# The first weight-block sum of an FFN Strassen pair, taken from VectorE and made by an adding DMA of GpSimd

## The chip, the core and the metric

The kernel runs on one core of a Trainium2 chip, in one launch. The metric is the device time in microseconds; the time before is the median of three runs.

## What is computed

One layer of a diffusion backbone over 512 latent tokens of width 2048 (float32): adaLN-modulated RMSNorm, an input projection into an S5 branch and a Hyena branch, their merge and the output projection, then the SwiGLU FFN, and a last RMSNorm. The change is in the FFN:

```python
def swiglu(h, w_in, w_out):
    a, b = jnp.split(h @ w_in, 2, axis=-1)
    return (jax.nn.silu(a) * b) @ w_out
...
        x = x + gate_mix[:, None] * mixer_output(u_x, y_x, hy_x, gates_x, lp)
        x = x + gate_ffn[:, None] * swiglu(modulate(x, norm_ffn[l], shift_ffn, scale_ffn),
                                           w_ffn_in[l], w_ffn_out[l])
```

## The kernel before

The work is written engine by engine, one function each for SP, GpSimd (POOL), ScalarE, VectorE and TensorE, with semaphores between them; the order on an engine is the order of its code. Every weight stands twice in a matmul: as a high half, rounded to fp32r by ScalarE, and as a low half, the difference, made by VectorE.

The first product of the FFN has 44 tiles of 128 columns for the gate (a) and as many for the up side (b). Tiles 0 to 2 are done plainly, the other 41 (`N_PAIR`) as **pairs**: gate and up tile of one number, cut with the 2048 rows of the contraction in halves, are a 2 x 2 grid of weight blocks of 128 x 1024 elements (512 KB), multiplied with a 2 x 2 grid of activation blocks by Strassen's scheme in Winograd's form, with seven block products in place of eight. A pair p so needs seven weight operands. Blocks 0, 1, 2 and 3 are loaded, and four sums are made of them:

- sum one, block 4 = block 3 + block 2 (L2097)
- sum two, block 3 = block 0 - block 3, in place (L2101)
- sum three, block 5 = block 4 - block 0 (L2104)
- sum four, block 6 = block 1 - block 5 (L2109)

`PRODUCTS = (0, 4, 5, 1, 3, 6, 2)` gives the block of each of the products 0 to 6. The seven operands of a pair lie in a ring of twelve buffers `wx`; `x_free(p, j)` is the count of finished products (`w_used`) from which the buffer of block j of pair p is free.

Who does what, while TensorE runs product i of pair p (o = 7p + i):

- **TensorE**, `pair_product` (L2839 to L2854): eight tiles of the contraction, for each a matmul of 512 columns with the high half (L2851) and one of 256 with the low half (L2853). It waits for the low half (`w_lo`) and, where a PSUM bank is used again, for ScalarE's copy of it.
- **ScalarE** makes the high half three products ahead (`operand_hi`, L1264), copies the banks of products 0, 1, 2 and 4 to SBUF (`chain_copy`, L1276), the last half bank of a pair (`up_half_copy`, L1281), and the SiLU (`pair_silu`, L1287).
- **VectorE** makes the low half two products ahead (`operand_lo`, L2115), and after it, at products 1 to 4, the four sums for pair p + 1 (`weight_sum`). In pair 0 the sums for pair 1 are at products 2, 3, 4 and 5. It also adds the banks up (L2122 to L2138), makes the low halves of the activation block sums `T` at the start (L2085), and at product 5 of pairs 0 to 31 does one row of the adaLN matrix (`ada_row`, L1651), which has nothing to do with the pairs.
- **SP** loads the blocks 3, 0, 2, 1 of a pair in this order (`pair_weights`, L596), each when its buffer is free and the sums of the pair before that read its own block of this number are done (`x_sum`). In the steady state these are the ends of products 2, 3, 5 and 6 of the pair two before.
- **POOL** multiplies SiLU and up side of a finished pair (`pair_product`, L812), stores the product to HBM (`store_act`, L806) and loads a row for `ada_row` when VectorE has done one (`ada_in`, L668), one after the other for each tile g.

In what follows T0 is the time at which product 0 of a pair starts.

Of the kernel before, what the change touches and what calls it, by code (L numbers as in the profile page):

```python
# [64 lines left out]
N_PLAIN = 3  # L65
N_PAIR = TILES - N_PLAIN
# [15 lines left out]
A_TILE = (0, 1, 3, 2)  # L82
# [16 lines left out]
MUL, ADD, SUB = ALU.mult, ALU.add, ALU.subtract  # L99
# [26 lines left out]
def block_kernel(nc, vecs_d, w_ac_d, w_ar_d, w_in_d, w_glu_d, w_hy_d, w_out_d, w_fi_d, w_fo_d, x_d, ctx_d,  # L126
# [5 lines left out]
    def at(name, off_kb, shape, dt=F32):  # L132
        return nc.alloc_sbuf_tensor_at(name, shape, dt, offset=base + int(off_kb * kb))
# [128 lines left out]
    wx = [at(f"wx{j}", o, [P, HU]) for j, o in enumerate(x_at)]  # L262
# [29 lines left out]
    def sem(name):  # L292
        return nc.alloc_semaphore(name)
# [1 line left out]
    s_vec, s_par, s_filt, s_dec, s_f3w, s_ctx = (sem(n) for n in  # L295
        ("vec_loaded", "s5a_loaded", "filter_loaded", "decay_loaded", "f3w_loaded", "ctx_loaded"))
    s_id, s_row = sem("ident_loaded"), sem("square_rows_ready")
    s_x, s_tabf = [sem(f"x_or_block_weight_loaded{g}") for g in range(4)], [sem(f"tabf_loaded{c}") for c in range(2)]
    s_pos = sem("postab_loaded")
    am_in = [sem(f"ada_mix_loaded{j}") for j in range(3)]  # L300
    am_used, am_row, am_cmb, ada1_used = (sem(n) for n in
# [3 lines left out]
    w_ld = [sem(f"hw_loaded{s}") for s in range(4)]  # L305
    w_hi, w_lo, w_used = sem("hw_hi_ready"), sem("hw_lo_ready"), sem("hw_used")
# [33 lines left out]
        "tf_loaded_or_xacc_moved", "tg_loaded_or_act_or_xacc_loaded"))  # L340
    tb_hi, tb_lo = sem("table_hi_ready"), sem("table_lo_ready")
    ut_ps, ut_h, ut_l = sem("uT_psum"), sem("uT_hi_ready"), sem("uT_lo_ready")
    pq_ps, pq_ev, k_in = sem("spec_psum"), sem("spec_free"), [sem(f"kf_in{j}") for j in range(2)]
    yv, yh, yl = sem("Y_ready"), sem("Y_hi_ready"), sem("Y_lo_ready")
    cv_ps, cv_out, od_cp, oh, ol = (sem(n) for n in ("conv_psum", "conv_gated", "odd_copied", "hyo_hi_ready", "hyo_lo_ready"))

# [6 lines left out]
    wz_free, x_sum = sem("pair_out_ready"), sem("h_or_weight_sum_ready")  # L353
# [23 lines left out]
    def ffn_slice(n):  # L377

        return w_fi_d[n - N_HU]

    def slot(n):

        return n % 3 if n < N_HU else (3, 1, 2, 0)[(n - N_HU) % 4]

    def x_buffer(p, j):

        return (7 * p + RING[j]) % 12

    def x_free(p, j):

        b = 7 * p + RING[j]
        if b < 12:
            return {1: N_HU + 9, 5: N_HU + 9, 6: N_HU + 10}.get(b, N_W if b > 6 else 0)
        return N_W + 7 * ((b - 12) // 7) + PRODUCTS.index(RING.index((b - 12) % 7)) + 1
# [63 lines left out]
    for c, x, i in D_FILL:  # L458
        n, blocked = DOWN.index((c, x, i)), CHUNKS[c][2]
        if not blocked or PRODUCTS[i] < 4:  # L460
            j = PRODUCTS[i] if blocked else n % 4
# [26 lines left out]
    w_loads = [sum(slot(i) == j for i in range(N_W)) for j in range(4)]  # L488

    with nc.Block() as block:  # L490
        @block.sync
        def _(sp):
# [64 lines left out]
            n = H_MRG + 2 * N_FILL  # L557
# [7 lines left out]
            def ffn_weights(n):  # L565

                if n == N_HU:
                    sp.wait_ge(m_sum, KT)
                else:
                    sp.wait_ge(w_used, n - 3)  # L570
                sp.dma_start(hw_raw[slot(n)][:, :], ffn_slice(n)).then_inc(w_ld[slot(n)], 16)

            def down_weights(n):

                c, x, i = DOWN[n]
                j, count, last = d_load[n]
                sp.wait_ge(w_used, d_free(n))
                landed = s_x[j] if CHUNKS[c][2] else w_ld[j]
                if last is None and not CHUNKS[c][2]:
                    sp.wait_ge(x_sum, 4 * N_PAIR + 4)  # L580
                if last is not None and CHUNKS[c][2]:
                    sp.wait_ge(x_sum, d_sums(*DOWN[last][:2]) + (2, 4, 1, 1)[j])
                if last is not None and not CHUNKS[c][2]:
                    sp.wait_ge(w_hi, N_D + last + 1)
                row = D_ROWS.index((c, x, (0, 1, 3, 2)[j] if CHUNKS[c][2] else i))
                sp.dma_start(dw[d_buffer(n)][:, 0:d_width(n)], w_fo_d[row][:, 0:d_width(n)]).then_inc(landed, 16)

            def pair_weights(p, j):

                if x_free(p, j):  # L590
                    sp.wait_ge(w_used, x_free(p, j))
                if p:
                    sp.wait_ge(x_sum, 4 * p + (2, 4, 1, 1)[j])
                else:
                    sp.wait_ge(w_hi, (N_W, N_W - 2, N_W - 1, N_W - 3)[j])
                sp.dma_start(wx[x_buffer(p, j)][:, :], w_fi_d[4 * (N_PLAIN + p) + A_TILE[j]]).then_inc(w_ld[j], 16)  # L596
# [5 lines left out]
                    ffn_weights(N_HU)  # L602
            for n in range(N_HU + 1, N_W):
                ffn_weights(n)
            for p in range(N_PAIR):
                for j in ((3, 0, 2, 1) if p else (3, 1, 2, 0)):
                    pair_weights(p, j)
            for c, (k0, nk, blocked) in enumerate(CHUNKS):
                for x in range(KT // 2 if blocked else KT):
                    for i in ([PRODUCTS.index(j) for j in (3, 0, 2, 1)] if blocked else [i for cc, xx, i in DOWN if (cc, xx) == (c, x)]):  # L610
                        down_weights(DOWN.index((c, x, i)))
# [8 lines left out]
        def _(pool):  # L620
# [4 lines left out]
            for st in range(8):  # L625
                cs, f, half = 1 - st // 4, st // 2 % 2, st % 2
# [181 lines left out]
            def pair_product(p):  # L808
# [2 lines left out]
                pool.wait_ge(wz_free, 2 * p + 2)  # L811
                pool.tensor_tensor(f_s[:, :], f_s[:, :], u_sum[:, :], MUL).then_inc(ft_rd, 1)  # L812

            def load_act(c, part):

                k0, nk = CHUNKS[c][0:2]
                a, b = 4 * part, min(4 * part + 4, nk)
                pool.dma_start(a_raw[:, a:b, :], act_d[:, k0 + a:k0 + b, :]).then_inc(act_in[part], 16)
# [12 lines left out]
            for g in range(TILES - 1):  # L831
                if g == TILES - 2:
                    stored(7)
                    pool.wait_ge(w_used, N_D - 6)
                    load_act(0, 0)
                if g >= N_PLAIN:
                    pair_product(g - N_PLAIN)
                store_act(g)
                if 2 <= g < 32:
                    ada_in(N_WIDE + g)  # L840
# [566 lines left out]
        def _(dve):  # L1407
# [127 lines left out]
            a, b, c, e, r = (rt6[:, j, :] for j in range(5))  # L1535
# [344 lines left out]
            for q in range(4):  # L1880
                n = H_MRG + 3 * q
# [50 lines left out]
            n, row = H_MRG + 2 * N_FILL, N_GATE  # L1932
# [59 lines left out]
            for m in range(KT):  # L1992
                n = H_OUT + 2 * m
# [93 lines left out]
            def operand(p, j):  # L2087

                return wx[x_buffer(p, j)][:, :]

            def weight_sum(p, e):

                if e == 0:
                    dve.wait_ge(w_ld[2], 16 * (w_loads[2] + p + 1))
                    dve.wait_ge(w_ld[3], 16 * (w_loads[3] + p + 1))
                    dve.wait_ge(w_used, x_free(p, 4))
                    tt(operand(p, 4), operand(p, 3), operand(p, 2), ADD).then_inc(x_sum, 1)  # L2097
                if e == 1:
                    dve.wait_ge(w_ld[0], 16 * (w_loads[0] + p + 1))
                    dve.wait_ge(x_sum, 4 * p + 5)  # L2100
                    tt(operand(p, 3), operand(p, 0), operand(p, 3), SUB).then_inc(x_sum, 1)  # L2101
                if e == 2:
                    dve.wait_ge(w_used, x_free(p, 5))
                    tt(operand(p, 5), operand(p, 4), operand(p, 0), SUB).then_inc(x_sum, 1)  # L2104
                if e == 3:
                    dve.wait_ge(w_ld[1], 16 * (w_loads[1] + p + 1))
                    dve.wait_ge(w_used, x_free(p, 6))
                    dve.wait_ge(x_sum, 4 * p + 7)
                    tt(operand(p, 6), operand(p, 1), operand(p, 5), SUB).then_inc(x_sum, 1)  # L2109
# [151 lines left out]
            for o in range(7 * N_PAIR):  # L2261
                p, i = o // 7, o % 7
                if o in (1, 3):
                    h_sums_lo((3, 1)[o // 2])
                if o + 2 < 7 * N_PAIR:
                    if p + 1 < N_PAIR and i == 5 and p == 0:
                        weight_sum(1, 3)
                    operand_lo(o + 2)
                else:
                    down_lo(o + 2 - 7 * N_PAIR)  # L2270
                e = i - 1 if p else i - 2
                if p + 1 < N_PAIR and 0 <= e < 4 and not (p == 0 and e == 3):
                    weight_sum(p + 1, e)
                if i == 0 and p == 33:
                    dve.wait_ge(ada1_used, 8 * KT)
                if p and i == 0:
                    up_folds(p - 1)
                if i == 4:
                    gate_sum(p, 0)
                if i == 5:  # L2280
                    if p < 32:
                        ada_row(N_WIDE + p)
                    if p == N_PAIR - 1:
                        for k in range(4):
                            act_lo(0, k)
                    up_sum(p)
                if i == 6:
                    gate_sum(p, 1)
                    gate_fold(p)
                if o == 1:  # L2290
                    ffn_product(2)
# [4 lines left out]
            for n, (c, x, i) in enumerate(DOWN):  # L2296
# [24 lines left out]
                if c < N_XC:  # L2321
                    e = n - D_FIRST[c] - 11
# [777 lines left out]
```

## Time and profile before

| what | us |
|---|---|
| median of 3 runs (lowest, highest) | 2776.66 (2776.16, 2777.51) |
| time of the profiled execution | 2776.75 |
| its span | 2774.9 |
| TensorE busy (share) | 2730.1 (98%) |
| VectorE busy | 2169.9 (78%) |
| ScalarE busy | 1141.0 (41%) |
| GpSimd busy | 371.1 (13%) |

The span runs from the first to the last instruction, the time is that of the whole execution. A busy share says how long an engine worked, not whether anything waited for it. That is in the waits, in the idle times before groups of instructions, and in the timelines of the engines side by side. HBM reads are 428 MB, writes 44 MB, 170 GB/s over the span.

### The profile page before, as it was taken

How to read it: one execution, taken by the hardware profiler on the slowest of the kernel's cores; microseconds unless marked ns; L12 is line 12 of the kernel's file. 1: busy time of each engine (PE TensorE's matmuls, PEld its weight loads, DVE VectorE, ACT ScalarE, POOL GpSimd, SP SyncE). 2: the span in 40 equal slices, each digit the busy share in tenths (PEclk: the TensorE clock that was granted, in tenths of full speed). 3: DMA queues.
4: the chain of work that ended last, by engine and by line, in shares of the span. 5: the costliest groups of instructions: out<-in, count | busy, mean ns of one | idle time of the engine just before them, and what ended most of it. 6: DMA issues, size and time to landing. Idle time of an engine off the chain costs nothing.

```text
span 2774.9 us, 39621 instructions
## 1 busy us (share of the span) xinstructions
PE 2730.1 (98%) x15602; PEld 2313.4 (83%) x15602; DVE 2169.9 (78%) x2986; ACT 1141.0 (41%) x1701; POOL 371.1 (13%) x544
## 2 busy tenths in 40 slices
PE   7999999999999999999999999999999999999998
PEld 2688888888888888788788888888888888998997
DVE  6555676887885685666789999999999887776877
ACT  4332333223443532222245555555555554453542
POOL 0001331001333100001100111111111111000001
PEclk9999999999999999999999999999999999999999
DMA  9736985346775645767644444444444336434432
GB/s 403 323 95 150 190 191 143 115 129 192 225 226 180 240 135 181 232 223 264 218 159 141 153 147 154 144 155 145 152 141 129 123 115 212 143 92 151 137 103 96
DMA packets 144540, 475.27 MB, mean 171 GB/s; under 512 B 24993, under 2 KB 29489, under 8 KB 140130
## 3 DMA queue, kind: packets, MB, share of 16 engines
q1 hardware_dynamic: 85570, 300.90, 33.7%
q0 software_dynamic: 49760, 157.67, 18.2%
q10 hardware_dynamic: 9024, 14.16, 1.4%
q8 instruction: 124, 2.03, 0.3%
q14 instruction: 62, 0.51, 0.1%
HBM read 428.14 MB, written 44.44 MB: 170 GB/s over the span
## 4 chain that ended last, share of the span: by engine, by line
PE 88%; DMA 5%; DVE 3%; ACT 2%; issue 1%; POOL 1%; SPq 0%; ACTq 0%; POOLq 0%; DVEq 0%
PE ps L2851 19%; PE ps L2555 11%; PE ps L2557 11%; PE ps L2556 11%; PE ps L2853 10%; PE ps L2902 3%; PE ps L2901 3%; PE ps L2900 3%; PE ps L2879 2%; PE ps L2880 2%; PE ps L2881 2%; PE ps L2572 2%; PE ps L2532 1%; DMA hw_raw<-in_w_in 1%; DMA hw_raw<-in_w_glu 1%; PE ps L2599 1%
## 5 line engine op out<-in xcount | busy, mean ns | idle before, releaser
L1416 DVE TENSOR_TENSOR hw_lo<-hw_raw,hw_hi 128x1024 fp32r<-128x1024 f32 x220 | 269.1, 1224 | 320.2 <-ACT hw_hi L870 319.0
L870 ACT ACTIVATE hw_hi<-hw_raw 128x1024 fp32r<-128x1024 f32 x220 | 232.5, 1058 | 683.2 <-DMA hw_raw<-in_w_in 463.3
L2851 PE MATMUL ps<-t_hi_lo,wx_hi 128*128 128x512 f32 x1312 | 412.0, 395 | 0.0
L2115 DVE TENSOR_TENSOR wx_lo<-wx,wx_hi 128x1024 fp32r<-128x1024 f32 x287 | 351.4, 1224 | 41.7 <-ACT wx_hi L1264 37.2
L2555 PE MATMUL ps<-h_hi,hw_hi 128*128 128x512 f32 x896 | 354.0, 395 | 0.7 <-DVE st_a L1680 0.5
L2557 PE MATMUL ps<-h_hi,hw_lo 128*128 128x512 f32 x896 | 349.4, 390 | 0.0
L2556 PE MATMUL ps<-h_lo,hw_hi 128*128 128x512 f32 x896 | 348.8, 389 | 0.0
L1264 ACT ACTIVATE wx_hi<-wx 128x1024 fp32r<-128x1024 f32 x287 | 302.1, 1053 | 105.3 <-PE ps L2853 98.2
L2851 PE MATMUL ps<-h_hi_lo,wx_hi 128*128 128x512 f32 x984 | 309.0, 395 | 0.0
L2853 PEld LDWEIGHTS ps<-t_hi_lo,wx_lo 128*128 128x128 f32 x1312 | 246.5, 188 | 58.3
L2853 PE MATMUL ps<-t_hi_lo,wx_lo 128*128 128x256 f32 x1312 | 257.7, 278 | 0.0
L2853 PEld LDWEIGHTS ps<-h_hi_lo,wx_lo 128*128 128x128 f32 x984 | 184.8, 188 | 43.7
L1313 ACT ACTIVATE dw_hi<-dw 128x768 fp32r<-128x768 f32 (+1 forms) x192 | 144.4, 753 | 157.8 <-PE ps L2881 126.8
L2851 PEld LDWEIGHTS ps<-t_hi_lo,wx_hi 128*128 128x128 f32 x1312 | 199.7, 189 | 0.0
L2169 DVE TENSOR_TENSOR dw_lo<-dw,dw_hi 128x768 fp32r<-128x768 f32 (+1 forms) x192 | 162.0, 845 | 48.0 <-ACT dw_hi L1313 47.2
L2555 PEld LDWEIGHTS ps<-h_hi,hw_hi 128*128 128x128 f32 x896 | 168.2, 188 | 37.3 <-issue 2.8
L2557 PEld LDWEIGHTS ps<-h_hi,hw_lo 128*128 128x128 f32 x896 | 168.2, 188 | 35.7
L2556 PEld LDWEIGHTS ps<-h_lo,hw_hi 128*128 128x128 f32 x896 | 168.4, 188 | 33.7
L2853 PE MATMUL ps<-h_hi_lo,wx_lo 128*128 128x256 f32 x984 | 193.3, 278 | 0.0
L2901 PE MATMUL ps<-blk_lo_hi,dw_hi 128*128 128x256 f32 x672 | 190.2, 283 | 0.0
L2902 PE MATMUL ps<-blk_lo_hi,dw_lo 128*128 128x256 f32 x672 | 190.2, 283 | 0.0
L2900 PE MATMUL ps<-blk_lo_hi,dw_hi 128*128 128x256 f32 x672 | 190.2, 283 | 0.0
(430 smaller groups left out, 5688.9 us busy)
## 6 DMA issues: line engine op xcount, KB each, us to landing
wx<-in_w_fi SPq DMA_DIRECT2D x164, 512.0 KB, 3.6
hw_raw<-in_w_in SPq DMA_DIRECT2D x128, 512.0 KB, 4.8
ada1m<-in_w_ar POOLq DMA_DIRECT2D x96, 512.0 KB, 4.7
ada_mix<-in_w_ac SPq DMA_DIRECT2D x16, 2048.0 KB, 13.0
dw<-in_w_fo SPq DMA_DIRECT2D x80, 384.0 KB, 3.1
ada1g<-in_w_ar POOLq DMA_DIRECT2D x32, 512.0 KB, 5.5
hw_raw<-in_w_glu SPq DMA_DIRECT2D x32, 512.0 KB, 4.5
hw_raw<-in_w_out SPq DMA_DIRECT2D x32, 512.0 KB, 4.5
```

What stands on the lines that cost most here:

```text
L870: act.activation(hw_hi[slot(n)][:, :], hw_raw[slot(n)][:, :], ACT.Copy).then_inc(w_hi, 1)
L1264: act.activation(wx_hi[o % 4][:, :], wx[x_buffer(p, j)][:, :], ACT.Copy).then_inc(w_hi, 1)
L1416: tt(hw_lo[s][:, :], hw_raw[s][:, :], hw_hi[s][:, :].bitcast(F32), SUB).then_inc(w_lo, 1)
L2115: tt(wx_lo[b][:, :], wx[b][:, :], wx_hi[o % 4][:, :].bitcast(F32), SUB).then_inc(w_lo, 1)
L2555: mm(out, wh(k), xh[:, k0 + k, :], start=first and k == 0, stop=False)
L2556: mm(out, wh(k), xl[:, k0 + k, :], start=False, stop=False)
L2557: ins = mm(out, wl(k), xh[:, k0 + k, :], start=False, stop=last and k == nk - 1)
L2851: mm(out[:, :], wh[:, P * k:P * k + P], both[:, :, k, :], start=opens and k == 0, stop=False, skip_group_check=True)
L2853: ins = mm(out[:, 0:CW], wl[:, P * k:P * k + P], xh[:, k, :], start=False, stop=k == ST - 1, skip_group_check=True)
L2900: mm(out, wh[:, w], b_hi[j][:, k, :], start=opens and k == 0, stop=False, skip_group_check=True)
L2901: mm(out, wh[:, w], b_lo[j][:, k, :], start=False, stop=False, skip_group_check=True)
L2902: ins = mm(out, wl[:, w], b_hi[j][:, k, :], start=False, stop=k == K_S - 1, skip_group_check=True)
```

## The change

Sum one of the pairs 1 to 40 leaves VectorE. SP loads block 2 a second time, into the buffer of block 4 (`first_addend`), behind the four blocks of the pair. POOL, when that has landed, issues a DMA of block 3 from HBM that adds to the same buffer (`second_addend`), ahead of the pair product and the store in its order. VectorE, where sum one stood, waits for that DMA and counts `x_sum` up itself. Blocks 2 and 3 are still loaded as before. Sums two to four of pairs 2 to 40 stand one product later, as they already did for pair 1. Two semaphores that were done with are used again.

```diff
+            def first_addend(p):
+
+                sp.wait_ge(w_used, x_free(p, 4))
+                sp.dma_start(wx[x_buffer(p, 4)][:, :], w_fi_d[4 * (N_PLAIN + p) + A_TILE[2]]).then_inc(s_tabf[0], 16)
+
             for p in range(N_PAIR):
                 for j in ((3, 0, 2, 1) if p else (3, 1, 2, 0)):
                     pair_weights(p, j)
+                if p:
+                    first_addend(p)
...
+            def second_addend(p):
+
+                pool.wait_ge(s_tabf[0], 16 + 16 * p)
+                pool.dma_start(wx[x_buffer(p, 4)][:, :], w_fi_d[4 * (N_PLAIN + p) + A_TILE[3]], accum_op=ADD).then_inc(k_in[1], 16)
+
...
+                if N_PLAIN - 1 <= g and g - N_PLAIN + 2 < N_PAIR:
+                    second_addend(g - N_PLAIN + 2)
                 if g >= N_PLAIN:
                     pair_product(g - N_PLAIN)
                 store_act(g)
...
             def weight_sum(p, e):
 
-                if e == 0:
+                if e == 0 and p:
+                    dve.wait_ge(w_ld[3], 16 * (w_loads[3] + p + 1))
+                    dve.wait_ge(k_in[1], 128 + 16 * p)
+                    dve.sem_inc(x_sum, 1)
+                if e == 0 and p == 0:
...
-                e = i - 1 if p else i - 2
+                e = i - 2
```

VectorE in pair 1, from the low half of product 3 on, before (`wx_lo` rows are low halves, `wx` rows are sums for pair 2, buffer numbers behind the names):

```order
L2115 TENSOR_TENSOR wx_lo_264<-wx_252,wx_hi_269 128x1024 [waits hw_hi_ready]
L2097 TENSOR_TENSOR wx_246<-wx_248,wx_249 128x1024 [waits hw_used,hw_loaded3,hw_loaded2]
L2115 TENSOR_TENSOR wx_lo_265<-wx_253,wx_hi_270 128x1024 [waits hw_hi_ready]
L2101 TENSOR_TENSOR wx_248<-wx_245,wx_248 128x1024 [waits h_or_weight_sum_ready,hw_loaded0]
L2115 TENSOR_TENSOR wx_lo_256<-wx_244,wx_hi_267 128x1024 [waits hw_hi_ready]
L2104 TENSOR_TENSOR wx_250<-wx_246,wx_245 128x1024 [waits hw_used]
L2115 TENSOR_TENSOR wx_lo_266<-wx_254,wx_hi_268 128x1024 [waits hw_hi_ready]
L2109 TENSOR_TENSOR wx_251<-wx_247,wx_250 128x1024 [waits h_or_weight_sum_ready,hw_used,hw_loaded1]
```

The same place in the changed kernel, where L2133 is the low half, L2119, L2122 and L2127 are sums two to four:

```order
L2133 TENSOR_TENSOR wx_lo_264<-wx_252,wx_hi_269 128x1024 [waits hw_hi_ready]
L2133 TENSOR_TENSOR wx_lo_265<-wx_253,wx_hi_270 128x1024 [waits hw_hi_ready]
L2133 TENSOR_TENSOR wx_lo_256<-wx_244,wx_hi_267 128x1024 [waits hw_loaded3,kf_in1_or_sum_added,hw_hi_ready]
L2119 TENSOR_TENSOR wx_248<-wx_245,wx_248 128x1024 [waits h_or_weight_sum_ready,hw_loaded0]
L2133 TENSOR_TENSOR wx_lo_266<-wx_254,wx_hi_268 128x1024 [waits hw_hi_ready]
L2122 TENSOR_TENSOR wx_250<-wx_246,wx_245 128x1024 [waits hw_used]
L2140 TENSOR_TENSOR gate_sums<-gate_sums,ps 128x512 [waits hw_used,ffn_a_copied_or_silu]
L2133 TENSOR_TENSOR wx_lo_257<-wx_245,wx_hi_269 128x1024 [waits hw_hi_ready,dve_chain]
L2127 TENSOR_TENSOR wx_251<-wx_247,wx_250 128x1024 [waits h_or_weight_sum_ready,hw_used,hw_loaded1]
```

The wait for the adding DMA (`kf_in1_or_sum_added`) now stands ahead of the low half of product 5, and each of the three sums behind one more low half.

POOL in the changed kernel, in three tiles of the steady state (L824 is the adding DMA, L819 the pair product, L813 the store, L675 the row load):

```order
L824 DMA wx_248<-in_w_fi 128x1024
L819 TENSOR_TENSOR ffn_silu<-ffn_silu,ct_201 128x512
L813 DMA act<-ffn_silu 128x512
L675 DMA ada1m_190<-in_w_ar 128x1024
L824 DMA wx_243<-in_w_fi 128x1024
L819 TENSOR_TENSOR ffn_silu<-ffn_silu,ct_201 128x512
L813 DMA act<-ffn_silu 128x512
L675 DMA ada1m_189<-in_w_ar 128x1024
```

Before, the rows were the same without L824: the adding DMA stands between the row load and the pair product.

## Rows read from the trace of the kernel before

**Rows 1.** Windows: us; busy (instructions) per engine; clock; DMA share; GB/s

```profile
core 0: us, PE busy (x) PEld busy (x) DVE busy (x) ACT busy (x) POOL busy (x), PEclk, DMA share, GB/s
1500.00:2298.00 798.00, 798.00 (x4584) 696.21 (x4583) 747.03 (x764) 418.71 (x540) 114.27 (x113) 1.00 0.44 144
```

**Rows 2.** Page, costliest groups: xcount | busy us, mean ns | idle before

```profile
L2851 PE MATMUL ps<-t_hi_lo,wx_hi 128*128 128x512 f32 x1312 | 412.0, 395 | 0.0
...
L2853 PE MATMUL ps<-t_hi_lo,wx_lo 128*128 128x256 f32 x1312 | 257.7, 278 | 0.0
```

**Rows 3.** Timeline of ScalarE in pair 21: start us, us, instruction [idle before <-releaser]

```profile
1908.29 0.38 ACT L1281 ACTIVATE up_half<-ps 128x256 f32<-128x256 f32 x1 [1.73 <-PE ps L2853]
...
1911.08 0.60 ACT L1276 ACTIVATE gate_sums<-ps 128x512 f32<-128x512 f32 x1 [0.94 <-PE ps L2853]
1911.57 1.05 ACT L1264 ACTIVATE wx_hi<-wx 128x1024 fp32r<-128x1024 f32 x1
1913.86 0.60 ACT L1276 ACTIVATE ct<-ps 128x512 f32<-128x512 f32 x1 [1.24 <-PE ps L2853]
...
1916.65 0.60 ACT L1276 ACTIVATE gate_sums<-ps 128x512 f32<-128x512 f32 x1 [1.24 <-PE ps L2853]
...
1922.22 0.60 ACT L1276 ACTIVATE ct<-ps 128x512 f32<-128x512 f32 x1 [1.73 <-PE ps L2853]
...
1927.80 0.38 ACT L1281 ACTIVATE up_half<-ps 128x256 f32<-128x256 f32 x1 [1.73 <-PE ps L2853]
```

**Rows 4.** Timeline of VectorE in pair 21

```profile
1909.65 1.23 DVE L2115 TENSOR_TENSOR wx_lo<-wx,wx_hi 128x1024 fp32r<-128x1024 f32 x1 [0.40 <-ACT wx_hi L1264]
1910.80 2.31 DVE L2097 TENSOR_TENSOR wx<-wx,wx 128x1024 f32<-128x1024 f32 x1
1913.04 1.21 DVE L2115 TENSOR_TENSOR wx_lo<-wx,wx_hi 128x1024 fp32r<-128x1024 f32 x1
1914.17 1.21 DVE L2101 TENSOR_TENSOR wx<-wx,wx 128x1024 f32<-128x1024 f32 x1
...
1922.36 1.28 DVE L1651 CUSTOM_DVE_ANT_0 ada1m<-ada1m,silu_row_m,mod_x 128x1024 f32<-128x1024 f32 x1
1923.57 0.08 DVE L1651 DVE_READ_ACCUMULATOR2_ANT mod_x<- 128x1 f32 x1
1923.57 0.69 DVE L2131 TENSOR_TENSOR ct<-ct,ct 128x512 f32<-128x512 f32 x1
1924.29 1.22 DVE L2115 TENSOR_TENSOR wx_lo<-wx,wx_hi 128x1024 fp32r<-128x1024 f32 x1
...
1925.43 0.68 DVE L2122 TENSOR_TENSOR gate_sums<-gate_sums,ps 128x512 f32<-128x512 f32 x1
1926.14 0.69 DVE L2126 TENSOR_TENSOR gate_sums<-gate_sums 128x512 f32<-128x512 f32 x1
```

**Rows 5.** Source line L2097: xcount: ns min/median/max, first and last start

```profile
L2097 DVE TENSOR_TENSOR wx<-wx,wx x41: 1221/2316/2328, 1489.0 to 2261.9; 128x1024 f32<-128x1024 f32 x41
```

**Rows 6.** Timeline of POOL in pair 21

```profile
1904.44 0.54 POOL L668 DMA_DIRECT2D ada1m<-in_w_ar  x1 [11.03 <-DVE mod_x L1651]
1910.22 1.81 POOL L812 TENSOR_TENSOR ffn_silu<-ffn_silu,ct 128x512 f32<-128x512 f32 x1 [5.24 <-ACT ffn_silu L1287]
```

**Rows 7.** SP's block loads at 1498 to 1501, then at 1908

```profile
L596 SPq DMA_DIRECT2D wx<-in_w_fi x4: 327/380/382, 1498.7 to 1500.0; - x4
...
DMA to landing us min/median/max: 4.0/5.4/6.7
...
L596 SPq DMA_DIRECT2D wx<-in_w_fi x1: 328/328/328, 1908.3 to 1908.3; - x1
...
DMA to landing us min/median/max: 3.6/3.6/3.6
```

**Rows 8.** DMA issues at 1700 to 2260: xcount, KB each, median us to landing

```profile
ada1m<-in_w_ar POOLq DMA_DIRECT2D x20, 512.0 KB, 3.8
```

**Rows 9.** Timeline of ScalarE in pair 0

```profile
1504.22 0.60 ACT L1276 ACTIVATE ct<-ps 128x512 f32<-128x512 f32 x1 [0.72 <-PE ps L2853]
```

**Rows 10.** Timeline of VectorE in pair 0

```profile
1505.51 1.23 DVE L2097 TENSOR_TENSOR wx<-wx,wx 128x1024 f32<-128x1024 f32 x1 [0.24 <-DMA wx<-in_w_fi]
1506.66 2.28 DVE L2085 TENSOR_TENSOR t_hi_lo<-t_raw,t_hi_lo 128x2048 fp32r<-128x2048 f32 x1
1508.86 1.22 DVE L2115 TENSOR_TENSOR wx_lo<-wx,wx_hi 128x1024 fp32r<-128x1024 f32 x1
```

More of the change, by code:

```diff
@@ L297, in block_kernel @@
     s_id, s_row = sem("ident_loaded"), sem("square_rows_ready")
-    s_x, s_tabf = [sem(f"x_or_block_weight_loaded{g}") for g in range(4)], [sem(f"tabf_loaded{c}") for c in range(2)]
+    s_x, s_tabf = [sem(f"x_or_block_weight_loaded{g}") for g in range(4)], [sem(n) for n in ("tabf_loaded0_or_sum_begun", "tabf_loaded1")]
     s_pos = sem("postab_loaded")
@@ L342, in block_kernel @@
     ut_ps, ut_h, ut_l = sem("uT_psum"), sem("uT_hi_ready"), sem("uT_lo_ready")
-    pq_ps, pq_ev, k_in = sem("spec_psum"), sem("spec_free"), [sem(f"kf_in{j}") for j in range(2)]
+    pq_ps, pq_ev, k_in = sem("spec_psum"), sem("spec_free"), [sem(n) for n in ("kf_in0", "kf_in1_or_sum_added")]
     yv, yh, yl = sem("Y_ready"), sem("Y_hi_ready"), sem("Y_lo_ready")
```

## The prediction

> **What bounds the kernel now.** I read the windows first, for the stretch of the FFN pairs, 1500 to 2298 us [rows 1]. TensorE is busy for 798.0 of 798 us at a granted clock of 1.00, the 2.4 GHz level, and VectorE for 747.0, 94%. The page's costliest groups agree: the pair stage's matmuls have 0.0 us of idle time before them [rows 2]. So in this stage nothing but TensorE's own pace sets the time. ScalarE's timeline gives that pace, since its copies start as products end [rows 3]: a pair begins at T0 = 1908.29, its products end at 1911.08, 1913.86, 1916.65 and so on, 2.787 us each, and the next pair begins at 1927.80, 19.51 us later. All 41 pairs take 800 us, a share of the program in which work on VectorE is worth something only if TensorE comes to wait for it.
>
> VectorE's timeline of the same pair shows how far ahead it is [rows 4]. The low half (L2115) for product 3 ends at 1910.88 and the product starts at 1916.65; the tightest is that of product 1 of the next pair, begun at 1924.29 and ready at 1925.51 for a start at 1930.59. The lead is 5.1 us at its least and 5.8 at its most. That is the cushion that any new wait on VectorE first eats.
>
> **What is removed.** 40 of the 41 sums of L2097, median 2.316 us; the quickest took 1.221 [rows 5]. GpSimd's product of 1.81 us starts at 1910.22 and the sum at 1910.80 [rows 4, 6], so some 1.1 us of each is the two engines beside one another. VectorE loses 40 x 2.3 = 92 us of its 2170 busy us. None of it lies on the path: TensorE had no wait to give back. I cost it at nothing; the cover is TensorE itself.
>
> **What is moved.** Sums two to four (L2101, L2104, L2109) of pairs 2 to 40 come one product later. The first product that needs one of them (block 5, product 2 of the next pair) starts 25.1 us after T0, and its sum would still be done before 1921. Alone this costs nothing. With it the column reduction L1651 and what stands behind it stay at much the same distance from TensorE.
>
> **What is added.** SP issues one more load per pair, POOL one adding DMA: 80 transfers of 512 KB, 42 MB. The stretch moves 144 GB/s at a DMA share of 0.44 [rows 1]; the share should come to about 0.6. Bandwidth is not the limit, latency is: the two transfers follow one another through a semaphore, and VectorE now waits for the second.
>
> The chain of a later pair, from its T0. SP sends the first addend right behind block 1, whose issue stands at T0, 1908.3, and which lands after 3.6 us [rows 7]. Four loads issued together land after 4.0 to 6.7 us of their own issues, 1498.7 to 1500.0, so at 1502.7 and 1506.7 [rows 7]: 1.35 us for each further one. The first addend is down at T0 + 5.2. POOL, waiting, issues the second. Call its time from issue to landing B. No row shows an adding DMA. Below it is bounded by a plain load from the same queue, 3.7 [rows 8], above by two whole loads in a row, 7.4, since the destination has to be read as well as the source. I take the middle, 5.5: the destination's bytes are read beside the source's, not after the whole of it. With 0.1 for the two semaphores the sum is there at X = 5.2 + 0.1 + 5.5 = T0 + 10.8.
>
> VectorE stands idle from about T0 + 5.6, when it has done the low half of product 4 (its high half is copied from 1911.57 to 1912.62 [rows 3]), until X. Behind the wait on VectorE stand, in this order, at the starting distances of [rows 4]: the low half of product 5, sum two, low half 6, sum three, a gate sum, low half 0, sum four, L1651, the up sum, and low half 1. That is 6 x 1.14 + 0.71 + 1.21 + 0.72 + 1.22 = 10.7 us. Product 1 of the next pair starts at T0 + 8 x 2.787 = 22.3. So TensorE waits if X is over **11.6**. At 10.8 it does not, by 0.8 us.
>
> What else stands behind: on POOL the pair product and its store, which move from T0 + 1.9 to about T0 + 6 and end near 8; ScalarE's copy at product 5 (T0 + 13.9 [rows 3]) needs that product, 6 us later. POOL's row load (L668) waits for L1651, which used to end 4 us before the next T0 [rows 4, 6] and now ends at X + 8.8 = T0 + 19.6. The load is then issued with block 1 and the first addend of the next pair and shares the DMA engines with them: one more 1.35, X = 12.15, 0.55 over the limit. That pair's own L1651 is late again, so the following row load falls behind the addend and X falls back. I reckon that half of the 30 pairs with a row load are touched, at 0.25 us on average: **+3.5**, an estimate from these rows. On SP, block 3 of the pair after next waits for the first sum's count, at X instead of T0 + 8.4, still half a pair before VectorE needs it.
>
> **The first pair** is different. Pair 0 starts at 1498.65 (product 1 ends at 1504.22 [rows 9]), and the four loads of pair 1 leave together at that moment [rows 7]. The first addend is the fifth: 1506.7 + 1.35 = 1508.1. The sum is there at 1508.2 + B, not at 1505.5 where L2097 starts now [rows 10]. Behind the wait VectorE has here also the low half of an activation block sum (L2085), 2.2 us from its start to the next [rows 10]: 2.2 + 6 x 1.14 + 0.71 + 1.21 + 0.72 + 1.22 = 12.9 until low half 8, which product 8 needs at 1498.65 + 22.3 = 1520.95. TensorE waits 1508.2 + B + 12.9 - 1520.95 = B + 0.15: 3.9 us with B at 3.7, **5.7** at 5.5, 7.6 at 7.4. This holds at every value of B.
>
> **Sum.** 5.7 + 3.5 = +9.2 on the profiled execution's 2776.75 us (span 2774.9), which is within 0.1 us of the median of the three runs, 2776.66: 2786. About 0.2%, 5.6 us, is what a measurement of this kernel can tell from no change.
>
> **The rivals.**
> *Not slower to be told* (0.31). The second read costs no more than another load's 1.35 us in a queue of loads, so B is 5.1, or less. Only pair 0 stalls, 3.9 to 5.3 us, and X is at most 5.2 + 0.1 + 5.1 = 10.4, with a row load in front 11.75, hardly over the limit: 2780.7 to 2782. For it: the write side is the same 512 KB, and the source is HBM either way. Against: the extra read is real, and so may be the descriptors that POOL writes for it. It decides at B = 5.2. The Trainium skill ("Collectives: The Full Stack", section "The bandwidth ceiling: the fold count and why AG ≠ RS ≠ AR") speaks for it: a DMA that adds isn't slowed by the add but by reading two sources through one ring, at half the rate. No run here shows that yet; by it the sum would be +5.3 and not +9.2.
> *Every pair waits* (0.24). B over 6.3 puts X over 11.6 in each pair. At the upper bound, 7.4, X = 12.7: 1.1 x 31 = 34 us in pairs 1 to 31; later pairs lack L1651, so their limit is near 12.7 and they just pass. With 7.6 for pair 0: 2818; with the row load's 1.35 on half of the pairs, some 2838. Nothing in the profile excludes it, and it is open upwards, since B is the one price that no row holds.
> *Faster* (0.03). A product has 8 x 768 columns, which at one a cycle of 2.4 GHz would take 2.56 us; it takes 2.787. If VectorE's traffic made the 0.23, taking 12% of it off 280 products would give 280 x 0.23 x 0.12 = 8 us, 2769. Against it: the interval is 2.787 in the products with a sum of 2.3 us on VectorE and in those without [rows 3, 4].
> *The case of the sum* has 0.42.
>
> **How the numbers follow.** The likeliest case gives 2786; its own range is 2782 to 2797. The range wanted for 8 in 10 starts below the second case, at 2779.5, and reaches into the third as far as B = 7.4 with some row loads, 2828; the rest of the third and the faster case, some 0.15, stay out. Faster by over 0.2%: 0.03. Within 0.2%: the second case and the edge of the first, 0.33. Slower: 0.64.
>
> **What would show it.** In the changed profile: L2097's counterpart x1 in place of x41 and VectorE's busy time near 2078 us; POOL's adding DMA x40 with a median landing, which is B (5.5; the cases part at 5.2 and 6.3); in pair 0 an idle time of VectorE near 1506 to 1513 and a wait of TensorE of some 5 us released by a low half; after it, in the row-load pairs, waits of TensorE under 1 us each and none from pair 32 on. POOL's product should start at about T0 + 6. If TensorE shows no wait in pair 0, my reading of the four loads is wrong; if its waits grow from pair to pair, the loop through L1651 and the row load is stronger than reckoned; a total under 2775 would mean that TensorE's pace hung on VectorE.

## The result, and the profile after

The changed kernel takes 2803.01 us in the median (2801.42 to 2805.61) beside 2776.41 for the kernel before in the same comparison: a ratio of 1.0101 (95% interval 1.0089 to 1.0113), some 27 us slower. The forecast was 2786, slower, with a range of 2779.5 to 2828. The profiled execution took 2805.61 us with a span of 2803.8, 28.9 more than before.

The windows of the pair stage in the changed kernel (columns as in [rows 1]; the second row is one pair, number 12, of those that came out long):

```profile
core 0: us, PE busy (x) PEld busy (x) DVE busy (x) ACT busy (x) POOL busy (x), PEclk, DMA share, GB/s
1500.00:2325.00 825.00, 804.81 (x4570) 697.60 (x4569) 672.40 (x720) 419.79 (x537) 139.33 (x153) 1.00 0.65 189
...
1746.30:1767.60 21.30, 19.96 (x113) 17.15 (x112) 15.94 (x19) 10.11 (x13) 3.35 (x4) 1.00 0.62 183
```

TensorE, which had no idle time there [rows 1], now has 20 us of it, at the same granted clock of 1.00, the 2.4 GHz level. VectorE went from 94% to 82% busy. The DMA share rose from 0.44 to 0.65. The costliest groups of the page say the same of TensorE and VectorE (L2869 and L2133 are L2851 and L2115 of before, [rows 2]):

```profile
PE 2738.3 (98%) x15602; PEld 2316.7 (83%) x15602; DVE 2098.9 (75%) x2946; ACT 1142.6 (41%) x1701; POOL 396.1 (14%) x584
...
L2133 DVE TENSOR_TENSOR wx_lo<-wx,wx_hi 128x1024 fp32r<-128x1024 f32 x287 | 371.1, 1305 | 141.4 <-issue 77.3
L2869 PE MATMUL ps<-t_hi_lo,wx_hi 128*128 128x512 f32 x1312 | 414.2, 397 | 10.7 <-DVE wx_lo L2133 10.7
```

What TensorE waits for is in the waits of 1480 to 2400 us (us in total, times, the longest): low halves, which is VectorE.

```profile
PE ps L2869 <- DVE wx_lo L2133: 18.0, 21, 4.5
PE ps L2869 <- ACT ct L1290: 2.0, 3, 0.7
```

The second row, three waits for a copy of ScalarE, is the low half too, as pair 12 below shows. These waits are a lower bound, since some of the time is booked on the weight loads and in longer matmuls. The pairs' lengths are exact: ScalarE copies the last half bank when a pair ends. Its copies by source line, first of the kernel before, then of the changed one (columns: count, ns min/median/max, first and last start):

```profile
L1281 ACT ACTIVATE up_half<-ps x41: 384/384/389, 1518.2 to 2298.4; 128x256 f32<-128x256 f32 x41
```

```profile
L1295 ACT ACTIVATE up_half<-ps x41: 384/384/388, 1525.1 to 2328.6; 128x256 f32<-128x256 f32 x41
```

From the end of pair 0 to the end of pair 40 it was 780.3 us, 40 times 19.51; now it is 803.5 (by the timelines, which give two decimals: 1518.16 to 2298.42 and 1525.09 to 2328.57). So the **pairs 1 to 40 cost 23.2 us**. Pair 0 itself took 25.9 us in place of 19.7, from TensorE's first matmul in it to ScalarE's first such copy: **6.2 us**. Together 29.4; the span is 28.9 longer, so 0.5 was won elsewhere.

**Pair 0** came as reckoned. POOL and VectorE:

```profile
1508.66 0.89 POOL L824 DMA_DIRECT2D wx<-in_w_fi  x1 [19.17 <-DMA wx<-in_w_fi]
1509.23 0.88 POOL L813 DMA_DIRECT2D act<-ffn_silu  x1
```

```profile
1504.58 1.22 DVE L2133 TENSOR_TENSOR wx_lo<-wx,wx_hi 128x1024 fp32r<-128x1024 f32 x1
1514.21 2.29 DVE L2099 TENSOR_TENSOR t_hi_lo<-t_raw,t_hi_lo 128x2048 fp32r<-128x2048 f32 x1 [8.41 <-issue]
1516.42 1.22 DVE L2133 TENSOR_TENSOR wx_lo<-wx,wx_hi 128x1024 fp32r<-128x1024 f32 x1
```

POOL waits for the fifth load and issues the adding DMA at 1508.66; VectorE stands still for 8.4 us until 1514.21, and the activation sum's low half comes ahead of the low half that TensorE needs [rows 10]. The label "issue" stands for a wait whose event the page doesn't tie to an instruction; here it is the adding DMA's landing.

**The price of the adding DMA**, B, is 5.5 us (POOL's DMAs into `wx`; the time to landing counts from the start of the issue):

```profile
L824 POOL DMA_DIRECT2D wx<-in_w_fi x40: 857/879/897, 1508.7 to 2295.3; - x40
...
DMA to landing us min/median/max: 5.3/5.5/6.6
```

**A calm pair and a long one.** Pair 16 begins at T0 = 1829.35, takes 19.51 us, and the pair behind it 19.54. Pair 12 begins at 1746.26, takes 21.37, and pair 13 takes 21.66. POOL's timeline in 16 and then in 12:

```profile
1829.67 0.54 POOL L675 DMA_DIRECT2D ada1m<-in_w_ar  x1 [11.44 <-DVE mod_x L1665]
1835.00 0.88 POOL L824 DMA_DIRECT2D wx<-in_w_fi  x1 [4.79 <-DMA wx<-in_w_fi]
1835.58 1.61 POOL L819 TENSOR_TENSOR ffn_silu<-ffn_silu,ct 128x512 f32<-128x512 f32 x1
...
1748.09 0.54 POOL L675 DMA_DIRECT2D ada1m<-in_w_ar  x1 [11.36 <-DVE mod_x L1665]
1754.98 0.88 POOL L824 DMA_DIRECT2D wx<-in_w_fi  x1 [6.36 <-DMA wx<-in_w_fi]
```

In pair 16 the first addend is down 5.4 us after T0 and the adding DMA is issued at T0 + 5.65. In pair 12 the row load leaves at T0 + 1.83, the first addend comes down only at T0 + 8.4, and the adding DMA is issued at T0 + 8.7. The source line of SP's first addend in that stretch shows its issue, at T0 + 0.8 in place of 0.4, and its landing:

```profile
L608 SPq DMA_DIRECT2D wx<-in_w_fi x1: 1363/1363/1363, 1747.0 to 1747.0; - x1
...
DMA to landing us min/median/max: 7.7/7.7/7.7
```

The same load of pair 16 was issued in 0.43 us and landed after 5.0.

VectorE in pair 12, from sum four of the pair before on:

```profile
1745.37 1.22 DVE L2127 TENSOR_TENSOR wx<-wx,wx 128x1024 f32<-128x1024 f32 x1
1746.50 1.28 DVE L1665 CUSTOM_DVE_ANT_0 ada1m<-ada1m,silu_row_m,mod_x 128x1024 f32<-128x1024 f32 x1
...
1760.40 1.23 DVE L2133 TENSOR_TENSOR wx_lo<-wx,wx_hi 128x1024 fp32r<-128x1024 f32 x1 [5.23 <-ACT wx_hi L1278]
1761.54 1.22 DVE L2119 TENSOR_TENSOR wx<-wx,wx 128x1024 f32<-128x1024 f32 x1
...
1767.94 1.28 DVE L1665 CUSTOM_DVE_ANT_0 ada1m<-ada1m,silu_row_m,vecs 128x1024 f32<-128x1024 f32 x1
```

Product 5 itself should have started at T0 + 13.9, and its low half is ready at 1761.63, T0 + 15.4. TensorE's first weight load and first matmul of it:

```profile
1761.74 0.30 PEld L2869 LDWEIGHTS ps<-h_hi_lo,wx_hi 128*128 128x128 f32 x2 [0.81 <-issue]
```

```profile
1761.77 0.70 PE L2869 MATMUL ps<-h_hi_lo,wx_hi 128*128 128x512 f32 x2 [0.64 <-ACT ct L1290]
```

The row names ScalarE's copy, which ran at that time (from 1761.17). But `pair_product` asks ahead of product 5 only for the second copy of the pair, made long before. The low half, done 0.1 us ahead of the weight load, is what ended the wait. The other two waits booked on that copy stand at product 5 of a late pair as well. The low half of product 1 of pair 13 comes 9.5 us after that of product 5, at 1769.86, as reckoned. So TensorE can wait at two products of a pair. Its waits, in the windows 1768 to 1773 (product 1 of pair 13) and 1780 to 1786 (product 5):

```profile
PE ps L2869 <- DVE wx_lo L2133: 0.8, 1, 0.8
```

```profile
PE ps L2869 <- DVE wx_lo L2133: 0.9, 1, 0.9
```

The loop can be read off VectorE's rows. L1665 begins at 1746.50, after T0, since the wait of the pair before ended late; its end sends the row load (1748.09). Sum four ended at 1746.59, also after T0, and SP's load of block 1 waits for its count, so the first addend behind it starts later too. Both make the sum late, 14.0 us after T0; VectorE starts the low half of product 5 at 1760.40, 0.1 us after the adding DMA landed; ScalarE's high half, which the row names, was done at 1759.44. L1665 then begins at 1767.94, again after the next T0 of 1767.62. In the before kernel it began 5.4 us ahead of the next T0 [rows 4].

Pair 32 is the last long one (20.17), behind the last L1665. Pairs 33 to 40 take 19.51 us each.

### The profile page after: what moved, and what is told of

Same layout as the page of the kernel before. It is cut to its first block, busy times and chain, and to the rows that moved or that the text cites. A ratio compares the mean times of both kernels' runs of the same rounds, so it can differ in the third digit from the quotient of the medians.

```text
span 2803.8 us, 39661 instructions
## 1 busy us (share of the span) xinstructions
PE 2738.3 (98%) x15602; PEld 2316.7 (83%) x15602; DVE 2098.9 (75%) x2946; ACT 1142.6 (41%) x1701; POOL 396.1 (14%) x584
## 4 chain that ended last, share of the span: by engine, by line
PE 81%; DVE 8%; DMA 5%; issue 3%; ACT 3%; POOL 0%; SPq 0%; DVEq 0%; ACTq 0%; POOLq 0%
PE ps L2869 15%; PE ps L2573 11%; PE ps L2575 11%; PE ps L2574 11%; PE ps L2871 7%; PE ps L2920 3%; PE ps L2919 3%; PE ps L2918 3%; PE ps L2898 2%; PE ps L2897 2%; PE ps L2899 2%; PE ps L2590 2%; DVE wx_lo L2133 1%; PE ps L2550 1%; DMA hw_raw<-in_w_in 1%
## 5 line engine op out<-in xcount | busy, mean ns | idle before, releaser
L1430 DVE TENSOR_TENSOR hw_lo<-hw_raw,hw_hi 128x1024 fp32r<-128x1024 f32 x220 | 269.2, 1224 | 320.2 <-ACT hw_hi L884 319.1
L2133 DVE TENSOR_TENSOR wx_lo<-wx,wx_hi 128x1024 fp32r<-128x1024 f32 x287 | 371.1, 1305 | 141.4 <-issue 77.3
L2869 PE MATMUL ps<-t_hi_lo,wx_hi 128*128 128x512 f32 x1312 | 414.2, 397 | 10.7 <-DVE wx_lo L2133 10.7
L2869 PE MATMUL ps<-h_hi_lo,wx_hi 128*128 128x512 f32 x984 | 310.9, 397 | 9.4 <-DVE wx_lo L2133 7.3
L2869 PEld LDWEIGHTS ps<-t_hi_lo,wx_hi 128*128 128x128 f32 x1312 | 199.6, 189 | 14.3 <-DVE wx_lo L2133 14.2
```

The source lines that it names most:

```text
L1430: tt(hw_lo[s][:, :], hw_raw[s][:, :], hw_hi[s][:, :].bitcast(F32), SUB).then_inc(w_lo, 1)
L2133: tt(wx_lo[b][:, :], wx[b][:, :], wx_hi[o % 4][:, :].bitcast(F32), SUB).then_inc(w_lo, 1)
L2869: mm(out[:, :], wh[:, P * k:P * k + P], both[:, :, k, :], start=opens and k == 0, stop=False, skip_group_check=True)
```

## The experiments

All ratios are to the kernel before, on the same chip and in the same comparison; "pairs 1 to 40" is by how much the 40 pairs took longer in the profiled execution than 780.3 us. First: which part of the change costs?

**The later place of the sums.**

```diff
-                e = i - 1 if p else i - 2
+                e = i - 2
```

> The kernel before, with sums one to four of pairs 2 to 40 one product later on VectorE, all four still made there and no DMA added. My theory (the time is lost in the wait for the adding DMA): nothing, 2776 to 2777, TensorE without a wait in the pairs. Rival (the later place of the sums is itself late for ScalarE or SP): a wait of TensorE in every pair, 0.2 us or more each, 2784 and up.

Measured: ratio 1.0007 (0.9997 to 1.0016), pairs 1 to 40 0.0 us, no wait of TensorE in them. Moving the sums costs nothing.

**Traffic or wait?** The first addend leaves earlier, ahead of block 2:

```diff
                 for j in ((3, 0, 2, 1) if p else (3, 1, 2, 0)):
+                    if j == 2 and p >= 2:
+                        first_addend(p)
                     pair_weights(p, j)
-                if p:
+                if p == 1:
                     first_addend(p)
```

> The changed kernel with the first addend issued by SP ahead of block 2 in place of behind block 1, from pair 2 on; its buffer is free by then. All transfers and the adding DMA stay. My theory: the first addend lands before T0, POOL issues the adding DMA right behind the row load or before T0, the sum is there before VectorE's wait at T0 + 5.6; only pair 0 costs, 6 to 7 us, +0.22 to 0.28%. Rival (traffic, or the adding DMA's cost for other loads): +0.6% or more, with waits in the later pairs.

Measured: ratio 1.0024 (1.0015 to 1.0033), pairs 1 to 40 0.0 us. TensorE has one wait, in pair 0:

```profile
PE ps L2871 <- DVE wx_lo L2135: 4.2, 1, 4.2
```

All 80 transfers and all adding DMAs are there; only the order on SP differs, and 23 us are gone. The cost of the later pairs is the latency of the chain, not the bytes that it adds. (The barest test of the traffic, the same transfers into spare buffers that nobody waits for, was not timed.) The adding DMAs were slower here than in the changed kernel, beside the row load and the blocks (DMA issues of pairs 2 to 31, 1540 to 2110 us; the last number is the median to landing), and TensorE waited for none of them, since they were issued about 1.8 us before T0 and had landed by T0 + 7.6 at the latest, well ahead of the limit measured below:

```profile
wx<-in_w_fi POOLq DMA_DIRECT2D x30, 512.0 KB, 8.2
```

**Pair 0 apart.** Pair 1's sum stays on VectorE:

```diff
-                if p:
+                if p >= 2:
                     first_addend(p)
...
-                if e == 0 and p:
+                if e == 0 and p >= 2:
```

> The changed kernel, but pair 1 keeps its sum one on VectorE as before; the adding DMA begins with pair 2. My theory (pair 0 costs 6 us by itself, and the later waits feed themselves through the row load, from whatever start): pair 0 costs nothing, the later pairs still some 12 to 22 us, 0.4 to 0.8% over before. Rival (the stall of pair 0 sets the later ones off): all gone, within 0.1% of before.

Measured: ratio 1.0083 (1.0068 to 1.0098). Pair 0 is back at 19.7 us, and pairs 1 to 40 cost 22.7, a little over what was expected (12 to 22). The later waits need no push from pair 0; the two parts add up to the changed kernel.

**Both edits.**

> Both edits before together: first addend ahead of block 2, and pair 1's sum on VectorE. 39 of 41 first sums are made by the adding DMA. My theory: no wait of TensorE in the pairs at all, within 0.1% of before (TensorE is the bound, so not faster either), with VectorE's busy time some 85 us under that of before. Rival of the traffic: +0.4% or more. Rival of a gain (TensorE's pace hangs on VectorE): under before by 0.2% or more.

Measured: ratio 1.0000 (0.9990 to 1.0009), pairs 1 to 40 +0.1 us. The pair stage of this kernel in windows, and its busy times on the page:

```profile
1500.00:2300.00 800.00, 800.00 (x4592) 697.91 (x4592) 667.93 (x725) 422.83 (x541) 159.07 (x152) 1.00 0.64 194
```

```profile
PE 2734.0 (98%) x15602; PEld 2314.3 (83%) x15602; DVE 2090.5 (75%) x2947; ACT 1142.1 (41%) x1701; POOL 415.9 (15%) x583
```

TensorE is busy throughout again, with a DMA share of 0.64. VectorE has 79 us less to do than before, and the time is the same within 0.1%: no gain from VectorE's relief can be seen, with TensorE as the bound.

Second: why so much more than the +3.5 reckoned for the later pairs?

**No row load.** 30 transfers left out, with VectorE's work in place:

```diff
-                if 2 <= g < 32:
-                    ada_in(N_WIDE + g)
...
-                dve.wait_ge(ada1_in[row_slot(r)], 16 * row_loads(r))
+                if r < N_WIDE + 2:
+                    dve.wait_ge(ada1_in[row_slot(r)], 16 * row_loads(r))
```

> The changed kernel without the row loads of GpSimd in the pairs (30 transfers of 512 KB); VectorE still reduces the old contents of the two buffers at the same places, so its work stays and the output is not the reference's. My theory (the row load, issued when L1665 ends, falls into the first addend's transfer and puts X over 11.6): X stays at T0 + 10.7 to 11.2 in all pairs, TensorE waits in pair 0 alone, 2782 to 2784. Rival (VectorE is short of time after the wait whatever the row load does): 2795 to 2803.

Measured: ratio 1.0033 (1.0020 to 1.0046); pair 0 +7.6 us, pairs 1 to 40 +2.7. The later pairs lost 20 of their 23 us with the row load. They were not quite free of waits, against the expectation, and that measures the limit. X, from here on, is the landing of the adding DMA after T0. It was 10.2 to 11.7, and where it was over 11.1 the next pair came out longer by the excess (X = 11.38 gave 0.28, 11.45 gave 0.35, 11.60 gave 0.48), less what the pair itself had been longer by (11.71 gave 0.26 behind 0.35). So the limit is near **11.1**, not the 11.6 of the sum. In pairs 32 to 39, without L1665 behind the wait, X = 11.62 gave nothing. The source lines of the first addend and of the adding DMA:

```profile
L608 SPq DMA_DIRECT2D wx<-in_w_fi x40: 328/425/1217, 1496.1 to 2265.8; - x40
...
DMA to landing us min/median/max: 4.3/4.6/7.7
```

```profile
L824 POOL DMA_DIRECT2D wx<-in_w_fi x40: 848/869/905, 1504.0 to 2270.3; - x40
...
DMA to landing us min/median/max: 5.2/5.5/6.1
```

B is that of the changed kernel. The first addend's median is 4.6 where it is 5.0 in the changed kernel, and the 7.7 here is pair 0's fifth load alone: the longest of the later pairs is 5.5. So the row load acts on the first addend and not on B.

**Half a row load.**

```diff
-                pool.dma_start(row_buffer(r)[:, :], w_ar_d[r]).then_inc(ada1_in[row_slot(r)], 16)
+                w = 512 if r >= N_WIDE + 2 else 1024
+                pool.dma_start(row_buffer(r)[:, 0:w], w_ar_d[r][:, 0:w]).then_inc(ada1_in[row_slot(r)], 16)
```

> The changed kernel with row loads of half the size (256 KB, the first 512 columns) from the second one of the pairs on; VectorE reduces full rows, the other half of old contents, so the output is not the reference's. My theory: the price follows the row load's bytes. Between the kernel with no row load (+0.33%) and the changed kernel (+1.0%): +0.45 to 0.75%. Rival (it is POOL's issue and the order of the queues, not the bytes): as the changed kernel, +0.95% or more.

Measured: ratio 1.0074 (1.0059 to 1.0089), pairs 1 to 40 +14.3 us, between 2.7 and 23.2: the price follows the row load's bytes.

**The row load behind the adding DMA** in POOL's order:

```diff
                     second_addend(g - N_PLAIN + 2)
+                if 3 <= g < 33:
+                    ada_in(N_WIDE + g - 1)
...
-                if 2 <= g < 32:
-                    ada_in(N_WIDE + g)
```

> The changed kernel with POOL's row load placed directly behind the adding DMA in its order, ahead of the pair product, in place of behind the store; all transfers and all of VectorE's work stay. My theory (the harm is done by the row load's share of the DMA engines while the first addend is on its way): the first addend lands near T0 + 5.1 in all pairs, the row load now shares with the adding DMA, so B rises from 5.5 to between 6 and 7, X = 11.5 to 12.3, TensorE waits up to 0.7 us in a pair but the waits do not grow from pair to pair: +0.35 to 0.6%, under the changed kernel's +1.0%. Rival (what counts is the row load at all, wherever it is beside either of the two): +0.9% or more.

Measured: ratio 1.0061 (1.0040 to 1.0083), pairs 1 to 40 +9.0 us, the longest pair 20.6. The size is at the upper edge of what was expected, but not by the expected way: B did not grow, the row load's own time did; and there were runs of up to six long pairs (11 to 16: 19.7 to 20.3). POOL's adding DMA and its row load (the latter from 1520 to 2110 us):

```profile
L824 POOL DMA_DIRECT2D wx<-in_w_fi x40: 851/879/913, 1504.0 to 2275.8; - x40
...
DMA to landing us min/median/max: 5.2/5.5/6.4
```

```profile
L675 POOL DMA_DIRECT2D ada1m<-in_w_ar x30: 560/851/882, 1527.5 to 2100.5; - x30
...
DMA to landing us min/median/max: 6.3/6.6/7.4
```

X was over 11.1 in 21 of the first 31 pairs, up to 12.7, because the first addend was slow (up to 6.3 us, median 5.2 in pairs 2 to 31 beside 4.6 in the kernel without row loads). The row load can't have done that directly: it leaves 5.5 to 7.7 us after T0, when the first addend is down. So some 6 of these 9 us are not explained.

**L1665 ahead of the wait**, in VectorE's idle time:

```diff
+                if i == 1 and 1 <= p < 32:
+                    ada_row(N_WIDE + p)
                 if i == 5:
-                    if p < 32:
+                    if p == 0:
                         ada_row(N_WIDE + p)
```

> The changed kernel with VectorE's column reduction L1665 of pairs 1 to 31 at product 1, in the idle time ahead of the wait, in place of product 5. My theory: the limit for X rises from 11.6 to 12.8, the row load is issued at about T0 + 8.5, behind the store, and no longer beside the first addend; the later pairs wait for nothing, and pair 0 costs 6 to 7 us: +0.22 to 0.3%. Rival (the row load now slows the adding DMA itself, X over 12.8, or block loads late): +0.5% or more.

Measured: ratio 1.0019 (1.0009 to 1.0028), pairs 1 to 40 +0.5. TensorE's one listed wait is that of pair 0:

```profile
PE ps L2871 <- DVE wx_lo L2133: 4.7, 1, 4.7
```

With all transfers and all of VectorE's work in place the loop is cut at its other end: the row load leaves near T0 + 9, and nothing of L1665 stands behind the wait. The edit does both at once, it raises the limit and moves the row load, and doesn't tell the two apart.

**A plain load for the adding DMA.**

```diff
-A_TILE[3]], accum_op=ADD).then_inc(k_in[1], 16)
+A_TILE[3]]).then_inc(k_in[1], 16)
```

> The changed kernel with a plain load in place of the adding DMA, so that block 4 is block 3 alone and the output is not the reference's; all waits as they were. My theory: B falls from 5.5 to 3.7 to 4.0, so X to about T0 + 9.2; pair 0 costs 4.5 us and no later pair anything: 2780.5 to 2783. Rival (the number of transfers and the wait as such, not the price of the second): near 2800.

Measured: ratio 1.0030 (1.0017 to 1.0043), pair 0 +5.3, pairs 1 to 40 +4.8. B:

```profile
L824 POOL DMA_DIRECT2D wx<-in_w_fi x40: 528/528/542, 1507.1 to 2273.6; - x40
...
DMA to landing us min/median/max: 3.6/3.8/4.6
```

So the add itself costs 1.7 us of landing time (5.5 against 3.8). Of these, 0.35 are POOL's longer issue (879 against 528 ns): the first 4 KB packet starts 1.58 us after the issue begins in place of 1.23 (medians over the 40). My "nothing in later pairs" was wrong here too: seven pairs came out longer, each behind one in which first addend and row load were on their way together and X went over 11.1 (11.2 to 13.1).

| kernel | ratio (interval) | pair 0 | pairs 1 to 40 |
|---|---|---|---|
| changed | 1.0101 (1.0089 to 1.0113) | +6.2 | +23.2 |
| later sums only | 1.0007 (0.9997 to 1.0016) | 0 | 0.0 |
| adding DMA from pair 2 | 1.0083 (1.0068 to 1.0098) | 0 | +22.7 |
| half row load | 1.0074 (1.0059 to 1.0089) | +7.3 | +14.3 |
| row load behind adding DMA | 1.0061 (1.0040 to 1.0083) | +6.3 | +9.0 |
| no row load | 1.0033 (1.0020 to 1.0046) | +7.6 | +2.7 |
| plain second load | 1.0030 (1.0017 to 1.0043) | +5.3 | +4.8 |
| first addend early | 1.0024 (1.0015 to 1.0033) | +6.0 | 0.0 |
| L1665 ahead of the wait | 1.0019 (1.0009 to 1.0028) | +7.3 | +0.5 |
| first addend early, from pair 2 | 1.0000 (0.9990 to 1.0009) | 0 | +0.1 |

No version beats the kernel before: TensorE's 800 us of products stand in all of them.

## Why the prediction was right in its direction and short in its size

The direction and the mechanism were right, the size was not: the added time is about three times the 9.2 us forecast. The measured 2803 lies outside the likeliest case's own range (2782 to 2797). The wide range holds it only because it was stretched for another case, B of up to 7.4, which did not come about; that is luck.

**The bound, and the zeros.** TensorE is the bound, the removed sums give nothing, the moved sums cost nothing: the later-sums kernel and the one with both edits show it, each within 0.1% of before. VectorE's relief was 71 us instead of 92: the sums' 1.1 us beside POOL's product were not removed but moved, for the product, now later, runs beside low halves in half of the pairs (mean of L2133 1305 ns, 1224 before, 20 us over all).

**B.** 5.5 was forecast and 5.5 measured; the case with B at 5.1 or less is out. To hit it to the tenth was in part luck: the lower bound was read as 3.7 where the row says 3.8 [rows 8], and that the middle is the place was a choice. The add costs 1.7 us over the plain load in its place (5.5 against 3.8) where I had taken 1.8. The Trainium skill ("Collectives: The Full Stack", section "The bandwidth ceiling: the fold count and why AG ≠ RS ≠ AR") says of the reducing step of a collective that it is slowed not by the add but by reading two sources, at half the rate. By the 1.35 us of a load's share that gave 5.1; this case's trace agrees with the rule in the packets, which last 328 ns each in the middle of an adding DMA and mostly 159 in a plain load. The landing is 0.4 us later than the rule's, and 0.35 of that is the longer issue.

**The first pair.** 5.7 forecast, 6.2 measured; over the kernels with the adding DMA in pair 0 it was 6.0 to 7.6.

**The later pairs** are the term of the sum that was mis-sized: +3.5 forecast, **+23.2** measured. The mechanism was the one named, the row load issued with the first addend; without it 20 of the 23 us are gone. The step that failed is its pricing, "half of the 30 pairs with a row load are touched, at 0.25 us on average" (which is 3.75 and not 3.5), in four points.

First the limit: 11.1, not 11.6, so that the margin of the bare chain was 0.3 and not 0.8 us; in pairs 33 to 39 of the changed kernel, without a row load, X was 10.8 to 11.4. The missing 0.5 can be found. I took the starts of products from ScalarE's copies, but the low half has to be there for the product's first weight load. For product 1 of pair 22 in the kernel before, which I had starting at 1930.59 (its first weight load, its first matmul, and ScalarE's copy):

```profile
1930.28 0.30 PEld L2851 LDWEIGHTS ps<-t_hi_lo,wx_hi 128*128 128x128 f32 x2
...
1930.38 0.63 PE L2851 MATMUL ps<-t_hi_lo,wx_hi 128*128 128x512 f32 x2
...
1930.58 0.60 ACT L1276 ACTIVATE gate_sums<-ps 128x512 f32<-128x512 f32 x1 [0.94 <-PE ps L2853]
```

The weight load is 0.3 us ahead of the copy. Another 0.1 passes from the low half's end to a weight load that waits for it (1761.63 to 1761.74 above), and 0.1 from the adding DMA's landing to VectorE's start (T0 + 14.0 to T0 + 14.1 in pair 12).

Second the row load's effect: reckoned with one more 1.35 us, first addend down at T0 + 6.55; in pair 12 it was 8.4, with issue to landing 7.7 us where pairs 33 to 39 have 4.6. The 1.35 came from loads in one queue [rows 7]; two queues at once shared worse. Some 0.9 of the 3.1 is SP's issue, 1.36 us in place of 0.43; issues of up to 1.2 us stand in the kernel without row loads too, so that part is not the row load's alone.

Third the way back: I let X fall back after one pair. It does not, since a late sum four also holds up the load of block 1, behind which the first addend stands, an edge that the prediction left out; in 16 of pairs 1 to 30 the row load left over 1 us after T0.

Fourth a second wait: I asked only when product 1 of the next pair waits, and from an X of some 12.2 on product 5 waits too, for the low half right behind the wait (13.9 for its start, less 0.4, less 1.3 for the low half), later by what product 1 had waited. In all 21 of the pairs 1 to 32 were longer, by 1.1 us on average, 20 of them in runs of four to seven (1 to 5, 11 to 14, 18 to 24, 29 to 32), where I had half of them at 0.25.

**The rivals.** "Every pair waits" was not it: its condition, B over 6.3, is not met, and pairs 6 to 10 and 33 to 40 show no wait of size; yet the total lies among that case's, under its 2818. "Not slower" fell with B = 5.5 and with the row load. "Faster" fell with the kernel with both edits: 79 us less on VectorE, ratio 1.0000.

What stays open: why a first addend and a row load issued 1 us apart take up to 7.7 and 6.8 us when four loads of one queue land 1.35 us apart. The half-size row load shows that bytes matter and the kernel with the row load second shows that the one in front is spared, but how the DMA engines share out two queues was not tried by itself. Nor is it known what slowed the first addends in that last kernel, where no row load ran beside them.

## What to carry to other kernels

A sum handed from an engine to a DMA takes the engine's time off and puts a latency chain on: count the chain (load, semaphore, issue, landing) from the event that frees the buffer to the waiting instruction, and subtract it from the lead that the waiting engine has, with all that stands behind the wait. Take the deadline from the waiting instruction itself and not from a later sign of it: here that was 0.3 us of a reckoned margin of 0.8. Where the margin left is under a microsecond, look for what in the queue behind the wait triggers a transfer into the same chain: such a loop feeds itself. For the later pairs the cure cost nothing, issuing the first transfer as soon as its buffer was free; but an engine that nobody waits for is not worth relieving.

## What the runs showed of the hardware

- An adding DMA of 128 x 1024 float32 from HBM into SBUF, issued by GpSimd: 5.5 us from issue to landing (5.3 to 6.6), against 3.8 for the plain one at the same place; 879 against 528 ns of GpSimd's issue, which is part of these times; 8.2 us beside two or three other loads; 328 against 159 ns for most 4 KB packets.
- A row load (plain, 512 KB) issued just behind an adding DMA lands after 6.6 us, where it took 3.8 by itself [rows 8]; the adding one stays at 5.5.
- VectorE's sum and GpSimd's product, both reading two tiles of SBUF, still cost VectorE 1.1 us or more where they meet, for both of its instructions seen here: before it was the first sum (2.3 us [rows 5]), now it is a low half. 20 of the 287 low halves took 2.3 to 3.0 us in place of 1.22, and their mean rose from 1224 to 1305 ns.
